# Second mixer: two linear-attention scores in one break of the weight stream, sparse-attention scores moved to the outputs' break

## The chip, the cores and the metric

One core of a Trainium2 chip runs the whole program; the other cores are idle. The metric is the device time of one execution in microseconds (us), less is better. TensorE (PE in the profile) multiplies, ScalarE (ACT) and VectorE (DVE) do the arithmetic between, GpSimd (POOL) prepares weights, and the SyncE queue (SP) streams weights in from memory.

## The reference

The model is two blocks of two layers each, on 256 tokens of width 1024. The first block has gated feed-forwards around an attention mixer. Each layer of the second block is a mixer of three branches and a squared-ReLU MLP:

```
z = rms_norm(x) @ w_in                      # split into the parts below
o_nsa = nsa_attention(...)                  # 8 heads, compressed + selected + windowed keys
o_gla = gated_linear_attention(...)         # 4 heads, decayed scores, state carried over tokens
o_mem = memory_attention(...)               # 4 heads into a memory of 256 tokens
merged = sum_b sigmoid(merge_b + b_merge) * (o_b @ w_branch[b])
x = x + merged @ w_out
x = x + square(relu(rms_norm(x) @ w_up)) @ w_down
```

The change touches only how the kernel orders work in this second mixer. In the gated linear attention the score of query i and key j is `sum_d q[i,d] k[j,d] exp(b[i,d] - b[j,d])` for j <= i, where b is the running sum of the log gates; the kernel computes it in 8 levels (pairs of tokens that lie 128, 64, ... 1 apart share a reference point), one matmul per level and head, and picks each score from its level by masks.

## The kernel before

**The stream.** All weights arrive as pieces of 128x1024 numbers through a ring (7 slots raw, 5 rounded). ACT rounds a piece (`hi`, L1352), POOL makes the rest (`lo`, L581), and PE multiplies every piece as three products, hi\*hi, hi\*lo and lo\*hi (L608 to L610), so that the result has fp32 accuracy. In the mixer a strip of 512 output columns consists of 4 pieces, and one piece is 12 matmuls of 512 columns. A strip accumulates in two PSUM banks, strip i in banks 2\*(i%2) and the next: so the two banks of strip i-1 lie idle during strip i, once they have been evicted.

**The breaks.** All other matmuls of the mixer stand between the pieces, in breaks. `mix2_work()` is a table written by hand: for each strip (the six `merge` strips, then `gr`) and each of its four pieces, the steps that follow the piece. Every engine's program walks the same table through `mix2_order()` and emits its own part of each step, so the table sets the order on PE, DVE and ACT at once; each engine's queue is in order.

**The steps.** `nsa_unit t` handles unit t of the sparse attention (17 of them, two heads each 64 wide, odd t and t+1 as a pair): PE makes the scores of a pair (`nsa_score`, lines of `pair_of_scores`, L852, into the banks SCORE = 4 and 5) at odd t, the transposes of unit t-1 (`turn_blocks`, L829, into bank TURNED = 6), and at even t the outputs of a pair (`nsa_outs`, L1186 and L839, into bank OUT = 7). DVE does in `nsa_unit t` at odd t: `minima(1)` on score bank 5, the copy of the transposed unit t-1 (`take_turned`, L2082), `minima(0)` on score bank 4 (both L2063), and `normalise` (L2070, L2074); at even t only the copy and `normalise`. `minima(0)` comes behind `take_turned` because it writes the slot that the transposes read.
`gla_unit hp t` handles the linear attention of head pair hp: t = 0, 1 are the two halves (4 levels each) of the scores of the first 128 tokens, t = 2, 3 those of the second 128 (8 instructions each, L1064), t = 2 with two more into TURNED (L1054). Both heads' scores go into the banks SCORE. `gla_out` (L1079, L1081) writes the outputs of a token tile into TURNED. DVE copies them out (L2352) and picks the scores (L2368). `decay hp i` prepares the decays on DVE and ACT.

**The waits.** `free[...]` in PE's program holds for each of the banks the semaphore that its last reader raises. So whoever writes SCORE next waits for `mn` (both minima) behind sparse scores, or for `gread` (the masks' picks) behind linear scores; whoever writes TURNED waits for `pt` (L2082) or `og` (L2352).

Of the kernel before, what the change touches and what calls it, by code (L numbers as in the profile page):

```python
# [19 lines left out]
P = 128  # L20
S = 256
MT = S // P
# [97 lines left out]
def mix2_work():  # L120
# [5 lines left out]
    gu = [[("gla_unit", hp, t) for t in range(5)] for hp in range(2)]  # L126
# [19 lines left out]
        ("rows", 2): ([nu[17]], [nu[18], gu[1][4]], [gla[3]], [gla[4], gla[5]]),  # L146
        ("rows", 0): (none, [gla[6]], [gla[7]], none),
        ("rows", 1): (none, none),
    }

# [440 lines left out]
def pe_program(M, V, sem):  # L591
# [5 lines left out]
    free = {0: None, 1: None, "turned": None, "out": None}  # L597
# [397 lines left out]
    def mix2(layer, c0, turn_next):  # L995
# [41 lines left out]
        def gla_score(hp, u):  # L1037
# [4 lines left out]
            wait_free(0)  # L1042
            wait_free(1)
# [3 lines left out]
            for hh, i in order:  # L1047
# [16 lines left out]
                t = pe.matmul(psum[:, SCORE[hh], i * P:i * P + P], lhsT, rhs, start=True, stop=True,  # L1064
                              skip_group_check=True)
            t.then_inc(sem["score"], 1)
            free[0] = free[1] = ("gread", 4 * nxt("gread"))
# [124 lines left out]
        for step in mix2_order():  # L1192
            what = step[0]
            if what == "strip":
                i, j = step[1:]
                name = names[i]
                if j == 0:
                    evicted(i)
                a_hi, a_lo = (y_hi, y_lo) if name in ("mk", "mv") else (h_hi, h_lo)
# [54 lines left out]
            elif what == "gla_unit":  # L1254
                hp, t = step[1:]
                if t in (2, 4):
                    gla_out(hp, t // 2 - 1)
                if t < 4:
                    gla_score(hp, t)
            elif what == "nsa":  # L1260
                nsa_step(step[1])
            elif what == "nsa_unit":
                t = step[1]
                if t == 0 or t % 2 and t < NSA_UNITS:
                    nsa_score(t)
                if t % 2 == 0 and t >= 4:
                    nsa_outs(t - 3)
                if 0 <= t - 1 < NSA_UNITS:
                    nsa_turn(t - 1)
            elif what == "rows":  # L1270
                b, i = step[1:]
                second = lambda: None
                if b == 2 and i == 0:
                    evicted(len(names))
# [579 lines left out]
def dve_program(M, V, sem):  # L1854
# [349 lines left out]
    def mix2(layer, c0, rstd):  # L2204
# [143 lines left out]
        def gla_unit(hp, t):  # L2348
            if t in (2, 4):
                m = t // 2 - 1  # L2350
                dve.wait_ge(sem["go"], nxt("go"))
                dve.tensor_copy(V.gqk[:, m, S * hp:S * hp + S], psum[:, TURNED, S:2 * S]).then_inc(sem["og"], 1)  # L2352
                n["og"] += 1
# [479 lines left out]
```

## Time and profile before

| | us |
|---|---|
| median of 3 runs | 1906.5 (1905.95 to 1906.9) |
| profiled execution | 1906.14, of which the span of its instructions 1904.6 |
| PE busy in the span | 1893.5 (99%) |
| POOL busy | 1563.4 (82%) |
| ACT busy | 1042.7 (55%) |
| DVE busy | 1029.4 (54%) |
| chain that ended last, PE's share | 96% |
| granted clock of PE | 1.0 |

A row of the timeline gives the start in us from the span's start, the duration, engine, line, operation, the tile written and the tiles read, and shapes; matmuls overlap in the pipeline, so it is the distance between starts that tells what one costs. `128*128`, `64*128` and `128*64` behind MATMUL are the rows and columns of the array that it uses. An fp32 matmul leaves two records where it runs as two passes, and the transposes one each. The two second mixers lie at about 1027 to 1228 us and 1486 to 1687 us of the span, up to the last branch; the part that the change touches is 1117 to 1212 us in the first and 1576 to 1671 us in the second.

### The profile page before, as it was taken

To read this page: it belongs to the slowest core of one execution; us is meant where nothing else is said; L and a number is where in the kernel's file an instruction comes from. 1 tells how busy PE (TensorE), PEld (TensorE's weight loads), DVE (VectorE), ACT (ScalarE), POOL (GpSimd) and SP (SyncE) were. 2 spreads that over 40 slices of the span, in tenths; PEclk is the share of its full clock that TensorE was granted. 3 is DMA by queue.
4 is the path that set the end of the run, shared out by engine and by line. 5 is a ranking of instruction groups with operands and counts; after the bars stand their busy time and mean duration, and the time that the engine had idled before them with its cause. 6 is when DMAs were issued, how large, how long until landed. Compare 5 with 4: busy or idle time off the path is not lost.

```text
span 1904.6 us, 26699 instructions
## 1 busy us (share of the span) xinstructions
PE 1893.5 (99%) x9356; PEld 1540.0 (81%) x9356; DVE 1029.4 (54%) x2621; ACT 1042.7 (55%) x1774; POOL 1563.4 (82%) x1136
## 2 busy tenths in 40 slices
PE   9999999999999999999999999999999999999999
PEld 7888777888888877788888877788888877788887
DVE  5438445444676745553453687547443477655553
ACT  6445666444644476554467444655446554556543
POOL 8988876988798877698879787779887968788986
PEclk9999999999999999999999999999999999999999
DMA  7665434666666543367657343456757533346664
GB/s 284 238 236 187 150 120 153 192 197 190 208 232 197 193 161 122 122 218 258 192 178 267 121 142 123 147 177 205 247 195 255 173 125 131 122 147 198 197 191 142
DMA packets 98385, 348.96 MB, mean 183 GB/s; under 512 B 13229, under 2 KB 13901, under 8 KB 97741
## 3 DMA queue, kind: packets, MB, share of 16 engines
q1 hardware_dynamic: 97676, 346.13, 54.9%
q8 instruction: 75, 1.23, 0.3%
q10 hardware_dynamic: 576, 1.14, 0.2%
q14 instruction: 58, 0.47, 0.1%
HBM read 346.17 MB, written 1.05 MB: 182 GB/s over the span
## 4 chain that ended last, share of the span: by engine, by line
PE 96%; DVE 2%; POOL 1%; ACT 0%; issue 0%; DMA 0%; SPq 0%; ACTq 0%; DVEq 0%
PE psum L608 29%; PE psum L610 28%; PE psum L609 28%; PE psum L829 1%; PE psum L839 1%; PE psum L677 1%; PE psum L852 1%; PE psum L1064 1%; POOL lo L581 1%; PE psum L819 1%; DVE psum L2024 1%; PE psum L875 0%; PE psum L916 0%; PE psum L726 0%; PE psum L1215 0%; PE psum L733 0%
## 5 line engine op out<-in xcount | busy, mean ns | idle before, releaser
L581 POOL TENSOR_TENSOR lo<-raw,hi 128x256 fp32r<-128x256 f32 (+2 forms) x1132 | 1563.2, 1404 | 328.1 <-ACT hi L1352 300.8
L1352 ACT ACTIVATE hi<-raw 128x1024 fp32r<-128x1024 f32 (+1 forms) x616 | 642.9, 1053 | 485.3 <-PE psum L610 446.3
L608 PE MATMUL psum<-hi,h_hi 128*128 128x512 f32 (+1 forms) x1600 | 634.2, 396 | 1.3 <-DVE h_lo L1913 0.9
L610 PE MATMUL psum<-hi,h_lo 128*128 128x512 f32 (+1 forms) x1600 | 622.1, 389 | 0.0
L609 PE MATMUL psum<-lo,h_hi 128*128 128x512 f32 (+1 forms) x1600 | 621.3, 388 | 0.0
L608 PEld LDWEIGHTS psum<-hi,h_hi 128*128 128x128 f32 x1600 | 301.3, 188 | 67.0 <-issue 3.4
L2024 DVE STREAM_TRANSPOSE psum<-big 32x128 f32<-32x128 f32 (+1 forms) x960 | 344.1, 358 | 14.2
L610 PEld LDWEIGHTS psum<-hi,h_lo 128*128 128x128 f32 x1600 | 300.5, 188 | 62.4
L609 PEld LDWEIGHTS psum<-lo,h_hi 128*128 128x128 f32 x1600 | 301.1, 188 | 57.7
L608 PE MATMUL psum<-hi,y_hi 128*128 128x512 f32 x832 | 328.4, 395 | 0.4 <-DVE y_lo L2033 0.4
L610 PE MATMUL psum<-hi,y_lo 128*128 128x512 f32 x832 | 324.6, 390 | 0.0
L609 PE MATMUL psum<-lo,y_hi 128*128 128x512 f32 x832 | 324.3, 390 | 0.0
L2033 DVE TENSOR_TENSOR y_lo<-psum,y_hi 128x512 fp32r<-128x512 f32 x76 | 51.0, 689 | 330.3 <-ACT y_hi L1478 330.1
L608 PEld LDWEIGHTS psum<-hi,y_hi 128*128 128x128 f32 x832 | 156.3, 188 | 35.9 <-issue 2.5
L610 PEld LDWEIGHTS psum<-hi,y_lo 128*128 128x128 f32 x832 | 156.3, 188 | 32.9
L609 PEld LDWEIGHTS psum<-lo,y_hi 128*128 128x128 f32 x832 | 156.5, 188 | 31.1
L1520 ACT ACTIVATE soft<-soft,small 128x128 f32<-128x128 f32 (+1 forms) x120 | 54.6, 456 | 129.9 <-DVE small L2063 109.0
L2012 DVE SCALAR_TENSOR_TENSOR big<-psum,small,big 128x256 f32<-128x256 f32 (+1 forms) x120 | 61.0, 551 | 86.8 <-ACT big L1468 86.8
L1468 ACT ACTIVATE big<-psum,small 128x256 f32<-128x256 f32 (+1 forms) x120 | 57.1, 528 | 53.8 <-PE psum L610 53.8
L1478 ACT ACTIVATE y_hi<-psum 128x512 fp32r<-128x512 f32 x76 | 42.7, 583 | 17.8 <-DVE psum L2024 17.6
L2082 DVE COPY soft<-psum 128x384 f32<-128x384 f32 (+2 forms) x68 | 35.4, 521 | 27.4 <-PE psum L829 27.4
L829 PE MATMUL psum<-consts,soft 128*128 128x128 f32 x188 | 34.3, 287 | 0.7 <-DVE soft L2074 0.7
(308 smaller groups left out, 1329.4 us busy)
## 6 DMA issues: line engine op xcount, KB each, us to landing
raw<-in_stream SPq DMA_DIRECT2D x608, 512.0 KB, 4.2
big<-in_w SPq DMA_DIRECT2D x14, 512.0 KB, 6.9
big<-in_post SPq DMA_DIRECT2D x6, 512.0 KB, 5.2
special<-in_b_merge SPq DMA_DIRECT2D x2, 1536.0 KB, 8.1
raw<-in_stream SPq DMA_DIRECT2D x8, 296.0 KB, 5.8
memkv<-in_mem_turned SPq DMA_DIRECT2D x2, 1024.0 KB, 6.0
big<-in_band SPq DMA_DIRECT2D x2, 768.0 KB, 6.7
big<-in_x_turned SPq DMA_DIRECT2D x2, 512.0 KB, 5.9
```

What stands on the lines that cost most here:

```text
L581: t = pool.tensor_tensor(M.lo[:, slot, w], M.raw[:, slot, w], f32(M.hi[:, slot_hi, w]), ALU.subtract)
L608: pe.matmul(out, lhs_hi, rhs_hi, start=start, stop=False)
L609: pe.matmul(out, lhs_hi, rhs_lo, start=False, stop=False)
L610: return pe.matmul(out, lhs_lo, rhs_hi, start=False, stop=stop)
L829: t = pe.transpose(psum[:, TURNED, i * P:i * P + P], soft[:, slot, 0, col:col + P], V.ident)
L1352: act.activation(M.hi[:, slot_hi, used], M.raw[:, slot, used], ACT.Copy).then_inc(sem["hi"], 1)
L1468: t = act.activation(act_s[:, m, :], psum[:, bank + m, 0:width], ACT.Silu if gated else ACT.Relu, scale=V.scale[:, m:m + 1])
L1478: act.activation(flat(y_hi[:, kt:kt + 2, :]), psum[:, bank + g, :], ACT.Copy).then_inc(sem["yhi"], 1)
L1520: t = act.activation(out, prob[:, w], ACT.Exp, scale=-1.0, bias=mn[:, i:i + 1], accum_out=total[:, i:i + 1])
L2012: t = dve.scalar_tensor_tensor(prod_s[:, m, :], psum[:, bank + m, col:col + width], V.scale[:, m:m + 1], act_s[:, m, :], ALU.mult, ALU.mult)
L2024: t = dve.transpose(dst[32 * b:32 * b + 32, :, :, 32 * a:32 * a + 32], src[32 * a:32 * a + 32, :, :, 32 * b:32 * b + 32])
L2033: dve.tensor_tensor(flat(y_lo[:, kt:kt + 2, :]), psum[:, bank + g, :], f32(flat(y_hi[:, kt:kt + 2, :])), ALU.subtract).then_inc(sem["ylo"], 1)
```

## The change

Four things change, in both second-mixer layers.

1. The five `gla_unit` steps of a head pair become three. Step m makes both halves of the scores of token tile m (16 instructions, 18 for m = 1) in one go, behind the outputs of tile m-1. They stand in the break behind the second piece of a strip, behind an odd `nsa_unit` in the same break. Four breaks of a head pair (pieces 0, 2 of two strips, with `gla_out` in the third) become two, and the breaks behind pieces 0 and 2 of these strips are gone.
2. The first half's scores go to SCORE as before. The second half's go to the idle pair of strip banks, `idle_banks(strip)`: PE waits until the strip before has been evicted, and the strip that comes next into these banks waits until DVE has picked the scores.
3. Sparse scores of units 5, 7, ... 15 move from the odd `nsa_unit` to the even one before it, between its outputs and its transposes. The odd units keep only their transposes on PE. DVE's order within a unit is as before.
4. The outputs of the second token tile of head pair 0 move from the break of `nsa_unit` 8 to that of `nsa_unit` 9, ahead of the transposes; those of head pair 1 stay.

```diff
@@ mix2_work
-        ("merge", 2): ([gu[0][0]], [nu[5]], [gu[0][1]], [nu[6]]),
-        ("merge", 3): ([gu[0][2]], [nu[7]], [gu[0][3]], [gu[0][4], nu[8], decay[1][0]]),
-        ("merge", 4): ([nu[9], decay[1][1]], [nu[10], decay[1][2]], [nu[11], decay[1][3]], [nu[12]]),
-        ("merge", 5): ([gu[1][0]], [nu[13]], [gu[1][1]], [nu[14]]),
-        "gr": ([gu[1][2]], [nu[15]], [gu[1][3]], [nu[16]]),
+        ("merge", 2): (none, [nu[5], gu[0][0]], none, [nu[6]]),
+        ("merge", 3): (none, [nu[7], gu[0][1]], none, [nu[8], decay[1][0]]),
+        ("merge", 4): ([gu[0][2], nu[9], decay[1][1]], [nu[10], decay[1][2]], [nu[11], decay[1][3]], [nu[12]]),
+        ("merge", 5): (none, [nu[13], gu[1][0]], none, [nu[14]]),
+        "gr": (none, [nu[15], gu[1][1]], none, [nu[16]]),
...
+def idle_banks(strip):
+
+    return 2 - 2 * (strip % 2), 3 - 2 * (strip % 2)
...
@@ pe_program, gla_score
             pe.wait_ge(sem["eb"], n["eb"])
-            wait_free(0)
-            wait_free(1)
+            banks = idle_banks(strip) if part else SCORE
+            if part:
+                evicted(strip + 1)
+                wait_free("idle")
+            else:
+                wait_free(0)
+                wait_free(1)
...
@@ pe_program, the steps
-                if t == 0 or t % 2 and t < NSA_UNITS:
+                if t in (0, 1, 3):
                     nsa_score(t)
                 if t % 2 == 0 and t >= 4:
                     nsa_outs(t - 3)
+                    if t + 1 < NSA_UNITS:
+                        nsa_score(t + 1)
                 if 0 <= t - 1 < NSA_UNITS:
                     nsa_turn(t - 1)
...
@@ dve_program, gla_unit
-                                              queries(psum[:, 4:6, i * P:i * P + P])))
+                                              queries(psum[:, bank:bank + 2, i * P:i * P + P])))
```

What PE runs for the first token tile of a head pair. Before, strip `merge 2`, with stream pieces at the dots (L1064 linear scores, L852 sparse scores, L829 transposes):

```order
L1064 MATMUL psum<-memkv,big 128x128 [waits s_mn,s_eb]
L1064 MATMUL psum<-memkv,big 128x128 x7
...
L852 MATMUL psum<-kT,qT 128x128 [waits s_gread,s_qk]
L852 MATMUL psum<-kT,qT 128x128
L852 MATMUL psum<-kT,qT 128x256 x2
L829 MATMUL psum<-consts,soft 128x128 [waits s_pt,s_prob]
L829 MATMUL psum<-consts,soft 128x128 x2
...
L1064 MATMUL psum<-memkv,big 128x128 [waits s_mn,s_eb]
L1064 MATMUL psum<-memkv,big 128x128 x5
```

Now, one break (L834 are the transposes and L1074 the linear scores in the new numbering, L613 the stream):

```order
L834 MATMUL psum<-consts,soft 128x128 [waits s_pt,s_prob]
L834 MATMUL psum<-consts,soft 128x128 x2
L1074 MATMUL psum<-memkv,big 128x128 [waits s_mn,s_eb]
L1074 MATMUL psum<-memkv,big 128x128 x7
L1074 MATMUL psum<-memkv,big 128x128 [waits s_z_merge,s_eb]
L1074 MATMUL psum<-memkv,big 128x128 x5
L1074 MATMUL psum<-big,kT 128x128 x2
L613 MATMUL psum<-hi,h_hi 128x512 [waits s_lo]
```

Three breaks have become one, and the first linear score now stands directly behind the transposes, still with its wait for `mn`.

The second token tile on PE. Before, strip `merge 3`, first break (L1079 is `gla_out`, L1054 the two additional scores):

```order
L1079 MATMUL psum<-big 128x128 [waits s_pt,s_z_gv,s_gread]
L1079 MATMUL psum<-big 128x128
L1064 MATMUL psum<-memkv,big 128x128 [waits s_gread,s_eb]
L1064 MATMUL psum<-memkv,big 128x128 x3
L1054 MATMUL psum<-memkv,big 128x128 [waits s_og]
L1064 MATMUL psum<-memkv,big 128x128 x4
L1054 MATMUL psum<-memkv,big 128x128 [waits s_rowtile]
```

Now (L1093 is `gla_out`, L1064 the two additional scores):

```order
L834 MATMUL psum<-consts,soft 128x128 [waits s_pt,s_prob]
L834 MATMUL psum<-consts,soft 128x128 x2
L1093 MATMUL psum<-big 128x128 [waits s_pt,s_z_gv,s_gread]
L1093 MATMUL psum<-big 128x128
L1074 MATMUL psum<-memkv,big 128x128 [waits s_mn,s_eb]
L1074 MATMUL psum<-memkv,big 128x128 x3
L1064 MATMUL psum<-memkv,big 128x128 [waits s_og]
L1074 MATMUL psum<-memkv,big 128x128 x4
L1064 MATMUL psum<-memkv,big 128x128 [waits s_rowtile]
L1074 MATMUL psum<-memkv,big 128x128 [waits s_z_merge,s_eb]
```

The transposes stand directly ahead of `gla_out`, which writes the same bank, and the first scores wait for `mn` where they waited for `gread`.

DVE around the same place. Before (L2352 copies the outputs, L2361 the two additional scores, L2368 picks):

```order
L2352 COPY big<-psum 128x256 [waits s_go]
L2361 COPY extra<-psum 128x256 [waits s_score]
L2368 COPY_PREDICATED big<-special,psum 128x2x64
...
L2063 ISA soft,small<-psum,consts 128x128 [waits s_pturn,s_score,s_gread]
...
L2082 COPY soft<-psum 128x384 [waits s_o,s_pturn]
L2063 ISA soft,small<-psum,consts 128x128 [waits s_pturn,s_score]
...
L2070 RECIPROCAL small<-small 128x2 [waits s_exp]
L2074 TENSOR_SCALAR soft<-soft,small,extra 128x128 [waits s_dve]
```

Now (L2104 is the copy of the transposes, L2085 the minima, L2092 and L2096 `normalise`, L2372 the copy of the outputs):

```order
L2104 COPY soft<-psum 128x384 [waits s_o,s_pturn]
L2085 ISA soft,small<-psum,consts 128x128 [waits s_pturn,s_score]
...
L2092 RECIPROCAL small<-small 128x2 [waits s_exp]
L2096 TENSOR_SCALAR soft<-soft,small,extra 128x128 [waits s_dve]
L2096 TENSOR_SCALAR soft<-soft,small,extra 128x256
L2372 COPY big<-psum 128x256 [waits s_go]
L2384 COPY extra<-psum 128x256 [waits s_score]
```

The copy of the outputs now stands behind the whole DVE part of the sparse unit in the same break.

## Rows read from the trace of the kernel before

**Rows 1.** The page, busy time, share and instructions by engine.
```profile
PE 1893.5 (99%) x9356; PEld 1540.0 (81%) x9356; DVE 1029.4 (54%) x2621; ACT 1042.7 (55%) x1774; POOL 1563.4 (82%) x1136
```

**Rows 2.** Who waited for whom, PE: total us, times, longest us.
```profile
PE psum L839 <- DVE soft L2082: 1.2, 2, 0.7
PE psum L829 <- DVE soft L2074: 0.7, 2, 0.4
...
PE psum L608 <- POOL lo L581: 0.4, 2, 0.2
```

**Rows 3.** Timeline of PE, a break with transposes alone: start, duration, what.
```profile
1106.88 0.39 PE L609 MATMUL psum<-lo,h_hi 128*128 128x512 f32 x1
1107.11 0.39 PE L610 MATMUL psum<-hi,h_lo 128*128 128x512 f32 x1
1107.34 0.49 PE L829 MATMUL psum<-consts,soft 128*128 128x128 f32 x3
...
1107.90 0.40 PE L609 MATMUL psum<-lo,h_hi 128*128 128x512 f32 x1
```

**Rows 4.** Timeline of PE, a break with sparse scores and transposes.
```profile
1110.21 0.39 PE L610 MATMUL psum<-hi,h_lo 128*128 128x512 f32 x1
1110.53 0.93 PE L852 MATMUL psum<-kT,qT 64*128 64x128 f32 x8
1111.38 0.55 PE L829 MATMUL psum<-consts,soft 128*128 128x128 f32 x3
...
1112.00 0.39 PE L609 MATMUL psum<-lo,h_hi 128*128 128x512 f32 x1
```

**Rows 5.** Timeline of PE, two breaks with linear scores alone (first token tile).
```profile
1121.49 0.39 PE L610 MATMUL psum<-hi,h_lo 128*128 128x512 f32 x1
1121.81 1.16 PE L1064 MATMUL psum<-memkv,big 64*128 64x128 f32 x16
1122.90 0.50 PE L608 MATMUL psum<-hi,h_hi 128*128 128x512 f32 x1
1123.24 0.39 PE L609 MATMUL psum<-lo,h_hi 128*128 128x512 f32 x1
...
1129.93 0.94 PE L1064 MATMUL psum<-memkv,big 64*128 64x128 f32 x12
1130.71 0.39 PE L1064 MATMUL psum<-big,kT 64*128 64x128 f32 x4
1131.03 0.50 PE L608 MATMUL psum<-hi,h_hi 128*128 128x512 f32 x1
```

**Rows 6.** Timeline of PE, outputs of the first tile, then scores of the second.
```profile
1137.92 0.60 PE L1079 MATMUL psum<-big 128*128 128x128 f32 x4
1138.46 0.71 PE L1064 MATMUL psum<-memkv,big 64*128 64x128 f32 x8
1139.05 0.37 PE L1054 MATMUL psum<-memkv,big 64*128 64x128 f32 x1
```

**Rows 7.** Timeline of PE and DVE, end of transposes and start of their copy.
```profile
1153.26 0.55 PE L829 MATMUL psum<-consts,soft 128*128 128x128 f32 x3
...
1153.85 0.56 DVE L2082 COPY soft<-psum 128x384 f32<-128x384 f32 x1 [0.80 <-PE psum L829]
```

**Rows 8.** Timeline of DVE, the DVE part of an odd sparse unit.
```profile
1144.62 0.55 DVE L2082 COPY soft<-psum 128x384 f32<-128x384 f32 x1
...
1145.63 0.08 DVE L2063 DVE_READ_ACCUMULATOR2_ANT small<- 128x1 f32 x1
...
1145.83 0.68 DVE L2074 TENSOR_SCALAR soft<-soft,small,extra 128x128 f32<-128x128 f32 x2
```

**Rows 9.** Timeline of DVE, the two scalings of unit 5, when they took longest.
```profile
1128.67 1.47 DVE L2074 TENSOR_SCALAR soft<-soft,small,extra 128x128 f32<-128x128 f32 x2
```

**Rows 10.** Timeline of DVE, the copy of the linear outputs.
```profile
1138.57 0.42 DVE L2352 COPY big<-psum 128x256 f32<-128x256 f32 x1 [0.88 <-PE psum L1079]
```

**Rows 11.** Timeline of PE, outputs of `nsa_unit` 12.
```profile
1169.68 0.88 PE L839 MATMUL psum<-soft,big 128*64 128x128 f32 x12 [0.49 <-DVE soft L2082]
```

More of the change, by code:

```diff
@@ L125, in mix2_work @@
     mu = [("mem_unit", t) for t in range(6)]
-    gu = [[("gla_unit", hp, t) for t in range(5)] for hp in range(2)]
+    gu = [[("gla_unit", hp, m) for m in range(MT + 1)] for hp in range(2)]
     decay = [[("decay", hp, i) for i in range(4)] for hp in range(2)]
@@ L595, in pe_program @@
     n = Counter()
-    free = {0: None, 1: None, "turned": None, "out": None}
+    free = {0: None, 1: None, "turned": None, "out": None, "idle": None}
     def nxt(name, k=1):
@@ L1035, in mem_out, with gla_score @@
             free["out"] = ("y2lo", nxt("y2lo"))
-        def gla_score(hp, u):
+        def gla_score(hp, u, strip):
             m, part = u // 2, u % 2
@@ L1063, in gla_score @@
                     lhsT, rhs = V.gla_k[hp][half, toks], V.gla_q[hp][half, toks]
-                t = pe.matmul(psum[:, SCORE[hh], i * P:i * P + P], lhsT, rhs, start=True, stop=True,
+                t = pe.matmul(psum[:, banks[hh], i * P:i * P + P], lhsT, rhs, start=True, stop=True,
                               skip_group_check=True)
             t.then_inc(sem["score"], 1)
-            free[0] = free[1] = ("gread", 4 * nxt("gread"))
+            read = ("gread", 4 * nxt("gread"))
+            if part:
+                free["idle"] = read
+            else:
+                free[0] = free[1] = read
             if u == 2:
@@ L1198, in mix2 @@
                     evicted(i)
+                    wait_free("idle")
+                    free["idle"] = None
+                    strip_now = i
                 a_hi, a_lo = (y_hi, y_lo) if name in ("mk", "mv") else (h_hi, h_lo)
@@ L1254, in mix2 @@
             elif what == "gla_unit":
[L1255 to L1259, printed above, removed]
+                hp, m = step[1:]
+                if m:
+                    gla_out(hp, m - 1)
+                if m < MT:
+                    for u in (2 * m, 2 * m + 1):
+                        gla_score(hp, u, strip_now)
             elif what == "nsa":
@@ L1273, in mix2 @@
                 if b == 2 and i == 0:
+                    wait_free("idle")
+                    free["idle"] = None
                     evicted(len(names))
@@ L2346, in taken, with gla_out, gla_unit @@
             dve.wait_ge(sem["gread"], nxt("gread"))
[L2348 to L2353, printed above, removed]
-            if t < 4:
-                part = t % 2
-                if hp == 0 and t == 0:
-                    own(dve.memset(V.att_flat, 0.0))
+        def gla_out(hp, m):
+            dve.wait_ge(sem["go"], nxt("go"))
+            dve.tensor_copy(V.gqk[:, m, S * hp:S * hp + S], psum[:, TURNED, S:2 * S]).then_inc(sem["og"], 1)
+            n["og"] += 1
+        def gla_unit(hp, step, strip):
+            if step:
+                gla_out(hp, step - 1)
+            if hp == 0 and step == 0:
+                own(dve.memset(V.att_flat, 0.0))
+            for part in range(2 if step < MT else 0):
+                bank = idle_banks(strip)[0] if part else SCORE[0]
                 dve.wait_ge(sem["score"], nxt("score"))
-                if t == 2:
+                if step and not part:
                     dve.tensor_copy(V.att_off_flat, psum[:, TURNED, 0:S])
@@ L2500, in mix2 @@
             what = step[0]
-            if what == "memory_in":
+            if what == "strip":
+                strip_now = step[1]
+            elif what == "memory_in":
                 for pair in (2 * step[1], 2 * step[1] + 1):
@@ L2563, in mix2 @@
             elif what == "gla_unit":
-                gla_unit(*step[1:])
+                gla_unit(*step[1:], strip_now)
             elif what == "nsa":
```

2 lines of the change are left out of this document (1 added, 1 removed).

## The prediction

> **What bounds the kernel now.** I read the page first: PE is busy 99% of the span [rows 1], so a step is worth what it adds to PE's queue, and the 54% of DVE matter only where PE waits. The list of waits came next: PE waits for DVE 1.9 us in four places and for POOL 0.4 us in two [rows 2]. So neither weights nor arithmetic hold PE up today, and there is next to nothing to win from waits; what can be won is PE's own time in the breaks. Then the timeline of PE through merge 2 to gr. A stream matmul follows the next by 0.23 us (1106.88, 1107.11) [rows 3]. I measure a break from the last stream matmul before it to the second one behind it, less two such steps (0.455 us), because the first matmul behind a break is always late. Last, the timeline of DVE beside it, for when a bank comes free. The same pattern stands 459 us later in the second layer, so I work out one layer and double it.
>
> **What the breaks cost by shape.** Transposes alone: 1107.90 - 1107.11 - 0.455 = 0.335 us [rows 3]. Sparse scores and transposes: 1112.00 - 1110.21 - 0.455 = 1.335 us, so the scores add 1.00 [rows 4]. Linear scores, half a tile: 1123.24 - 1121.49 - 0.455 = 1.295 us [rows 5]. Inside, a pair of records (two heads side by side) takes 0.11 us: six pairs take 0.78, two pairs and the way back to the stream 0.32, all eight 1.09 to 1.10 [rows 5]. That is 8 x 0.111 = 0.89 plus 0.1 in and 0.1 out; the rest of 1.295 lies in the stream matmuls on either side, 0.32 instead of 0.23 before and 0.34 instead of 0.23 behind. So every change between the full array and half of it costs about 0.2 us.
>
> **What the change removes, per layer.**
> - The second half of the linear scores follows the first without a change of shape: it adds 0.89 instead of 1.295. Four times (two tiles, two head pairs): 4 x 0.405 = 1.6 us.
> - The first half, behind transposes instead of in its own break: 0.23 + 0.33 (three transposes) + 0.10 + 1.09 + 0.34 - 0.455 = 1.63, and apart 0.335 + 1.295 = 1.63. Nothing. The 0.10 is the change of shape behind outputs: four records from 1137.92, scores at 1138.46, 0.54 = 4 x 0.11 + 0.10 [rows 6].
> - Six sparse scores (units 5 to 15) stand between outputs and transposes. From their first record to the transposes is 1111.38 - 1110.53 = 0.85 us [rows 4], where they cost 1.00 in a break with the transposes: 6 x 0.15 = 0.9 us. The outputs use half the columns (128\*64), the scores half the rows (64\*128), and no break of today puts these two side by side. I take the same 0.2 us for that change as rows 5 give for one to the full array. Bounds: no change at all, 0.65 each and 1.2 us more won; twice the price, 1.2 us less.
> - The outputs of tile 1 of pair 0 move from one break to the next with no change of shape on either side: nothing.
>
> Together 2.5 us a layer, with bounds 1.3 and 3.7. For the sparse scores the Trainium skill has a rule, TensorEngine Tiling (Array Packing), Key Properties: going to another tiling mode drains the array, going to another tile of the same mode does not. Rows 5 agree (0.2 us in and out, none between the heads' halves), and by the rule the untried change from columns to rows drains too, which is the 0.9 us; without a drain that term would be 2.1 us.
>
> **What it adds: waits in the same break.** Today a bank written by one break is read by DVE during the next pieces. The change puts writer and next writer side by side. I set 0 at the last stream matmul before the break.
>
> (c) Tile 0, twice a layer. The transposes start at 0.23 and the linear scores could start at 0.66. They write bank 4, which holds the sparse scores of unit 6 (14) until `minima(0)`, and DVE does `minima(0)` behind the copy of these very transposes. The transposes end 0.49 behind their start [rows 3], at 0.72; the copy starts 0.04 later (1153.81, 1153.85) [rows 7], at 0.76; the minima end 1.09 behind the start of the copy (1144.62, 1145.63 + 0.08) [rows 8], at 1.85; PE follows 0.06 us behind DVE (copy to 1138.99, L1054 at 1139.05) [rows 6, 10]. So the scores start at 1.91: a wait of 1.25 us. Bounds 1.0 (the first of the accumulators suffices) and 1.35.
>
> (a) Tile 1, twice a layer, three waits in a row. `gla_out` writes the bank of the transposes: it may start when their copy is done, 0.76 + 0.55 + 0.06 = 1.37 instead of 0.56, a wait of 0.81. Its scores then start at 1.37 + 0.54 = 1.91, just when the minima are done. The additional scores L1054 come 0.59 behind (1138.46, 1139.05) [rows 6], at 2.50, and need the copy of the outputs. But DVE's queue has the copy of the outputs behind `normalise`: scalings from 0.76 + 1.21 = 1.97 [rows 8], which last 0.68 to 1.47 us [rows 8, 9]; I take the middle, next start at 2.98. Copy 0.42 and 0.06: 3.46, a wait of 0.96 (0.55 to 1.4). Together 1.77, bounds 1.36 and 2.2.
>
> (b) `nsa_unit` 9, once a layer. Its transposes stand directly behind `gla_out` and need its copy: outputs end, 0.04 to the copy, 0.42, 0.06, so 0.53 from 1138.52 to 1139.05 [rows 6, 10], where they would have followed 0.16 before that end: 0.69 us. Today sparse outputs of 0.8 us lie between and hide it. DVE's decays of pair 1 (four operations behind `nsa_unit` 8) end about when the outputs do; bounds 0.55 and 1.0.
>
> What does not wait: the second half's idle banks (the strip before is evicted over 5 us earlier), the next strip in them (DVE needs some 7 us from the break's start for all picks, PE comes back after 9), and the scores moved ahead of the transposes (their banks' minima are two pieces old).
>
> (d) `nsa_unit` 12 waits today for DVE, whose decays fill its queue: 0.49 us for a copy in layer 0 [rows 11], and then for the scalings, 1.9 us over both layers [rows 2]. The chain of DVE through units 8 to 11 stays as it is, some 0.6 us later by (b); the sparse scores now lie between outputs and transposes and hide the second of these waits. I take 1.0 us off for both layers together; bounds 0 and 1.9.
>
> **The sum.** 2 x (2 x 1.25 + 2 x 1.77 + 0.69 - 2.5) - 1.0 = 2 x 4.23 - 1.0 = 7.5 us. The profiled execution took 1906.14 us (span 1904.6): 1913.6; the median of the runs is 0.4 us higher. I say 1913.5 us, 0.4% slower. All low bounds: 2 x (2.0 + 2.72 + 0.55 - 3.7) - 1.9 = 1.2 us; all high: 2 x (2.7 + 4.4 + 1.0 - 1.3) = 13.6 us.
>
> **Rivals.**
> 1. Faster, 1899 us. DVE's answers cost PE nothing: the point is whether `minima(0)` and the copies are done before the next writer's turn. If DVE had them by then, only the 2.5 us a layer and the 1.9 us of today's waits would be left, 2 x 2.5 + 1.9 = 6.9 us. For it: DVE is idle nearly half of the time, and it would be enough to have another piece between. Against: the copy needs the transposes of the same break, and PE's queue is in order. Chance 0.07.
> 2. No change, 1907 to 1910. The waits are there but short: the change from outputs to scores does not drain (2.4 us less), scalings take 0.68 us (0.4 less, four times), and today's waits go altogether. 7.5 - 2.4 - 1.6 - 0.9 = 2.6 us, 1908.7. For it: six places with an unseen change of shape. Chance 0.20.
> 3. Slower by more, 1917 to 1920: DVE, pushed back by (b), delays the outputs of unit 12 more than now, then the transposes of unit 13 (it has some 0.4 us to spare there), and the scores behind them; with 1.5 us in each of two places a layer, 7.5 + 4 to 6. Chance 0.10.
> 4. The second half cannot use the idle banks in time and waits for the eviction or its reader: then the merged break is split by a wait of up to the 1.4 us of the eviction. Nothing in the order makes DVE late there. Inside the others' chances.
>
> **The numbers.** Forecast 1913.5 with chance 0.63 for 1910 to 1917. About 0.2% (3.8 us) is what a measurement of this kernel can tell from no change. Slower: 0.63 and 0.10, of which I move 0.03 to the middle for its lower end, 0.70. Same: 0.20 and 0.03, 0.23. Faster: 0.07. The range 1905.5 to 1917.5 leaves out the first rival and most of the third.
>
> **What would show it.** In the new profile PE's waits for DVE grow from 1.9 to some 14 us: the linear scores wait 1.2 us for L2085 (minima) twice a layer, `gla_out` 0.8 us for L2104, L1064 about 1 us for L2372, the transposes of unit 9 some 0.5 us for L2372. The step between a linear score pair stays 0.11 us throughout the merged break, there are 8 breaks fewer a layer, and the sparse scores take 0.85 us between outputs and transposes. If PE's waits stay near 2 us, the forecast is wrong and the first rival right. POOL and ACT keep their order and lead; a wait of PE for `lo` would be a cause I did not count.

## The result, and the profile after

The changed kernel takes 1915.59 us, the median of six runs, against 1906.24 us for the kernel before in as many runs on the same chip. The ratio is 1.005, interval [1.004, 1.006]: slower by 9.35 us, where 7 us were forecast. The six runs lie in two groups: 1913.93, 1913.96 and 1914.27 us with a granted TensorE clock of 1.0, and 1916.90, 1917.37 and 1917.78 us with a mean clock of 0.998. The profiled execution is the slowest of them (1917.78 us, span 1916.3), so a part of what its trace shows beyond the one before is the clock, told of below.

The page, busy time by engine. It answers to [rows 1]:

```profile
PE 1894.9 (99%) x9356; PEld 1544.2 (81%) x9356; DVE 1029.7 (54%) x2621; ACT 1043.1 (54%) x1774; POOL 1563.6 (82%) x1136
```

The numbers of instructions are those of before, and so are the busy times within 1.4 us (4.2 on PEld). The span is 11.7 us longer, so about 10 us are time in which PE stands idle. (Its share still reads 99%: 12 us are 0.6% of the span.)

The list of waits of PE, against [rows 2]: who waited for whom, total us, times, longest:

```profile
PE psum L1074 <- issue: 5.0, 4, 1.2
PE psum L1093 <- DVE soft L2104: 3.0, 4, 0.7
PE psum L1064 <- DVE big L2372: 2.1, 4, 0.9
PE psum L834 <- DVE big L2372: 1.2, 2, 0.6
PE psum L844 <- DVE soft L2104: 1.1, 2, 0.6
...
PE psum L613 <- POOL lo L586: 0.4, 2, 0.2
```

These five are 12.4 us, where the prediction had some 14; before, the waits for DVE in this part were 1.9 us. Each stands at the place the prediction gave it. The first is the wait (c) and is put down to "issue", since the profile sees no releaser; DVE's timeline below shows that it ends with the minima. The wait for `lo` is unchanged: POOL has no part in it.

Timeline of PE and DVE, first token tile of head pair 0 in the first layer:

```profile
1125.66 0.39 PE L615 MATMUL psum<-hi,h_lo 128*128 128x512 f32 x1
1125.90 0.49 PE L834 MATMUL psum<-consts,soft 128*128 128x128 f32 x3
...
1126.42 0.56 DVE L2104 COPY soft<-psum 128x384 f32<-128x384 f32 x1 [2.46 <-PE psum L834]
...
1127.45 0.08 DVE L2085 DVE_READ_ACCUMULATOR2_ANT small<- 128x1 f32 x1
...
1127.63 1.83 PE L1074 MATMUL psum<-memkv,big 64*128 64x128 f32 x28 [1.25 <-issue]
...
1129.62 0.50 PE L613 MATMUL psum<-hi,h_hi 128*128 128x512 f32 x1
```

The reader is to see the chain: transposes end, copy 0.56, minima, last accumulator read at 1127.45 + 0.08, first score 0.10 later. The wait is 1.25 us. From the first score to the stream are 1.99 us for 32 records; the second half follows the first without a pause, though it writes other banks.

Second token tile of the same head pair:

```profile
1142.60 0.39 PE L615 MATMUL psum<-hi,h_lo 128*128 128x512 f32 x1
1142.83 0.49 PE L834 MATMUL psum<-consts,soft 128*128 128x128 f32 x3
...
1144.06 0.68 PE L1093 MATMUL psum<-big 128*128 128x128 f32 x4 [0.74 <-DVE soft L2104]
1144.58 1.13 DVE L2096 TENSOR_SCALAR soft<-soft,small,extra 128x128 f32<-128x128 f32 x2
...
1145.63 0.41 DVE L2372 COPY big<-psum 128x256 f32<-128x256 f32 x1
1146.09 0.37 PE L1064 MATMUL psum<-memkv,big 64*128 64x128 f32 x1 [0.70 <-DVE big L2372]
...
1146.97 0.42 PE L1064 MATMUL psum<-memkv,big 64*128 64x128 f32 x1
...
1147.18 0.42 PE L1064 MATMUL psum<-memkv,big 64*128 64x128 f32 x1
...
1149.24 0.79 PE L613 MATMUL psum<-hi,h_hi 128*128 128x512 f32 x1
```

Both waits of (a) are there, 0.74 us for the copy of the transposes and 0.70 us for the copy of the outputs, which starts only when the scalings (1.13 us) are through. And something that was not forecast: behind the second wait a pair of score records takes 0.21 us (1146.97 to 1147.18) where it took 0.11 before [rows 5]. The view by stretches shows why; PEclk is the third number from the end (width, then busy time and instructions of PE, PEld, DVE, ACT and POOL, PEclk, DMA share, GB/s):

```profile
1143.00:1146.00 3.00, 1.65 (x15) 1.12 (x13) 2.61 (x9) 1.84 (x5) 2.86 (x5) 1.00 0.49 182
1146.00:1149.00 3.00, 2.91 (x28) 2.91 (x28) 1.30 (x6) 0.09 (x1) 2.86 (x5) 0.58 0.00 0
1149.00:1152.00 3.00, 3.00 (x14) 2.29 (x13) 1.90 (x5) 0.00 (x0) 0.21 (x1) 0.85 0.00 0
...
1609.00:1612.00 3.00, 2.06 (x25) 1.87 (x24) 1.36 (x4) 1.12 (x3) 2.86 (x5) 0.79 0.18 71
1612.00:1615.00 3.00, 3.00 (x20) 2.55 (x19) 2.66 (x8) 0.00 (x0) 1.47 (x3) 0.64 0.02 5
```

A mean clock of 0.58 and then 0.85 means that (0.42 + 0.15) x 3 / 0.5 = 3.4 us were run at the lower of its two levels, 1.2 instead of 2.4 GHz. Before it, PE was busy 1.65 of 3.00 us. The same place of the second layer has it too, (0.21 + 0.36) x 3 / 0.5 = 3.4 us. Nowhere else in the second mixers, and nowhere there in the kernel before, does the clock fall.

The second token tile of head pair 1, at full clock:

```profile
1198.60 0.39 PE L615 MATMUL psum<-hi,h_lo 128*128 128x512 f32 x1
...
1200.06 0.68 PE L1093 MATMUL psum<-big 128*128 128x128 f32 x4 [0.74 <-DVE soft L2104]
...
1200.58 0.67 DVE L2096 TENSOR_SCALAR soft<-soft,small,extra 128x128 f32<-128x128 f32 x2
1201.16 0.42 DVE L2372 COPY big<-psum 128x256 f32<-128x256 f32 x1
...
1201.63 0.37 PE L1064 MATMUL psum<-memkv,big 64*128 64x128 f32 x1 [0.24 <-DVE big L2372]
...
1203.49 0.50 PE L613 MATMUL psum<-hi,h_hi 128*128 128x512 f32 x1
```

Here the scalings take 0.67 us and the wait is 0.24. (POOL had ended its last `lo` operation at 1200.30, while such operations ran beside the scalings of 1.13 us; experiment 1 has more on this.) From L1064 to the stream are 1.86 us; in the tile of head pair 0, most of it at half clock, 3.15. That difference, 1.29, and 0.32 more until the stream is back in its step of 0.23 are 1.6 us for each fall.

Last, the sparse scores, now between outputs (L844) and transposes (unit 6):

```profile
1135.30 0.88 PE L844 MATMUL psum<-soft,big 128*64 128x128 f32 x12
1136.11 0.93 PE L857 MATMUL psum<-kT,qT 64*128 64x128 f32 x8
1136.97 0.55 PE L834 MATMUL psum<-consts,soft 128*128 128x128 f32 x3
```

0.86 us from scores to transposes; 0.85 was forecast. This step has a change from half the rows to the full array, as in [rows 4]. The change that no break of before had, from half the columns to half the rows, lies one step earlier, from outputs to scores: 1136.11 - 1135.30 = 0.81 us. In the same unit of the kernel before, the outputs went straight to the transposes, from half the columns to the full array:

```profile
1133.97 0.88 PE L839 MATMUL psum<-soft,big 128*64 128x128 f32 x12
1134.78 0.55 PE L829 MATMUL psum<-consts,soft 128*128 128x128 f32 x3
```

That is 0.81 us too. So the unseen change costs what the one to the full array costs, as the forecast assumed.

### The profile page after: what moved, and what is told of

Its sections match the earlier page's. It is cut to its first block, busy times and chain, and to the rows that moved or that the text cites. A ratio compares the mean times of both kernels' runs of the same rounds, so it can differ in the third digit from the quotient of the medians.

```text
span 1916.3 us, 26709 instructions
## 1 busy us (share of the span) xinstructions
PE 1894.9 (99%) x9356; PEld 1544.2 (81%) x9356; DVE 1029.7 (54%) x2621; ACT 1043.1 (54%) x1774; POOL 1563.6 (82%) x1136
## 3 DMA queue, kind: packets, MB, share of 16 engines
q8 instruction: 75, 1.23, 0.3%
## 4 chain that ended last, share of the span: by engine, by line
PE 95%; DVE 3%; ACT 1%; issue 1%; POOL 1%; ACTq 0%
PE psum L613 28%; PE psum L615 28%; PE psum L614 28%; PE psum L834 1%; PE psum L844 1%; PE psum L682 1%; PE psum L857 1%; PE psum L1074 1%; POOL lo L586 1%; PE psum L824 1%; DVE psum L2046 1%; PE psum L880 0%; PE psum L921 0%; PE psum L731 0%; PE psum L738 0%
## 5 line engine op out<-in xcount | busy, mean ns | idle before, releaser
L613 PE MATMUL psum<-hi,h_hi 128*128 128x512 f32 (+1 forms) x1600 | 632.9, 396 | 1.3 <-DVE h_lo L1935 0.9
L613 PEld LDWEIGHTS psum<-hi,h_hi 128*128 128x128 f32 x1600 | 301.2, 188 | 67.4 <-issue 3.9
L613 PE MATMUL psum<-hi,y_hi 128*128 128x512 f32 x832 | 328.1, 394 | 0.4 <-DVE y_lo L2055 0.4
L613 PEld LDWEIGHTS psum<-hi,y_hi 128*128 128x128 f32 x832 | 156.2, 188 | 36.1 <-issue 2.5
L2104 DVE COPY soft<-psum 128x384 f32<-128x384 f32 (+2 forms) x68 | 35.5, 522 | 53.2 <-PE psum L834 53.2
L2096 DVE TENSOR_SCALAR soft<-soft,small,extra 128x128 f32<-128x128 f32 x64 | 34.6, 582 | 1.2
```

Of the source, the lines that this page charges most:

```text
L613: pe.matmul(out, lhs_hi, rhs_hi, start=start, stop=False)
L2104: dve.tensor_copy(soft[:, slot, 1, 0:width], psum[:, TURNED, 0:width]).then_inc(sem["pt"], 1)
```

## The experiments

All eight kernels compute the whole reference. I give the median and the ratio to the kernel before, which took 1906.2 to 1906.4 us in the runs made beside them. Where a break is compared, it is measured as in the prediction, or by its gap: from the last stream matmul before it to the first behind it, less one step of 0.23.

**1. The pairs in a break of their own.** The rival of the whole story is that the merged break or the new order of the sparse scores is itself slow. This kernel keeps the merged pairs, gives them a break of their own, the first of their strip, and puts the sparse scores back where they were.

```diff
-        ("merge", 2): (none, [nu[5], gu[0][0]], none, [nu[6]]),
-        ("merge", 3): (none, [nu[7], gu[0][1]], none, [nu[8], decay[1][0]]),
-        ("merge", 4): ([gu[0][2], nu[9], decay[1][1]], ...
+        ("merge", 2): ([gu[0][0]], [nu[5]], none, [nu[6]]),
+        ("merge", 3): ([gu[0][1]], [nu[7]], none, [gu[0][2], nu[8], decay[1][0]]),
+        ("merge", 4): ([nu[9], decay[1][1]], ...
...
-                if t in (0, 1, 3):
+                if t == 0 or t % 2 and t < NSA_UNITS:
                     nsa_score(t)
                 if t % 2 == 0 and t >= 4:
                     nsa_outs(t - 3)
-                    if t + 1 < NSA_UNITS:
-                        nsa_score(t + 1)
```

("merge", 5) and "gr" are changed in the same way.

> Both halves of the linear scores in one break with the second half in the idle strip banks, as in the changed kernel, but in a break of their own behind the strip's first piece; sparse scores in the odd units and the second tile's outputs in unit 8's break, as before the change. Theory (the halves together win 0.4 us each, the loss comes from waits that the new neighbours bring): four merges a layer of 0.405 us, no new wait, so 2 x 1.6 = 3.2 us under the kernel before: 1903.0 us, PE's waits for DVE near today's 1.9 us, granted clock 1.0 throughout. Rival (the merged break or the idle banks are themselves what costs): about as slow as the changed kernel, or at least not under 1906.

Measured: 1904.88 us (1904.69 to 1905.70, 11 runs), ratio 0.9993 [0.9984, 1.0001]; the interval just reaches no change. So the waits come from the place, not from the merging: against the changed kernel 10.7 us go. But only 1.5 of the 3.2 us of savings arrive. The merged break has the expected size; the rest is in new waits around unit 11:

```profile
PE psum L834 <- DVE soft L2094: 2.1, 4, 0.7
PE psum L844 <- DVE soft L2102: 1.4, 2, 0.7
```

DVE did not come earlier with PE. Its timeline, with the four decays behind unit 8:

```profile
1154.48 3.02 DVE L2351 TENSOR_TENSOR big<-extra 128x256 f32<-128x256 f32 x4
1157.42 0.28 DVE L2083 CUSTOM_DVE_ANT_0 soft<-psum,consts 128x128 f32<-128x128 f32 x1
```

and the same rows of the kernel before:

```profile
1155.52 1.95 DVE L2331 TENSOR_TENSOR big<-extra 128x256 f32<-128x256 f32 x4
1157.43 0.29 DVE L2063 CUSTOM_DVE_ANT_0 soft<-psum,consts 128x128 f32<-128x128 f32 x1
```

DVE starts its decays 1.04 us earlier, and they take 3.02 instead of 1.95 us and end at the same time, 1157.42. POOL's `lo` operations run without a pause until 1156.19 in the kernel before and 1156.88 here, so three of the four decays start beside them instead of one. Two more groups of four in the kernel before, the first with POOL at work and the second without:

```profile
1100.41 3.58 DVE L2331 TENSOR_TENSOR big<-extra 128x256 f32<-128x256 f32 x4
...
1159.80 1.43 DVE L2331 TENSOR_TENSOR big<-extra 128x256 f32<-128x256 f32 x4
```

All 32 decays of that kernel fall into two kinds: the 22 that start with no `lo` operation running take 0.41 or 0.42 us, the ten that start beside one 0.94 to 0.96. In experiment 1 it is 18 and 14, with the same times. No experiment removed POOL's work, but the rows leave no decay that goes the other way.

**2. The pairs one piece later.** The order of the sparse scores as in the change, but one piece of the stream between transposes and linear scores, and likewise between `gla_out` and unit 9.

```diff
-        ("merge", 2): (none, [nu[5], gu[0][0]], none, [nu[6]]),
-        ("merge", 3): (none, [nu[7], gu[0][1]], none, [nu[8], decay[1][0]]),
-        ("merge", 4): ([gu[0][2], nu[9], decay[1][1]], [nu[10], decay[1][2]], ...
-        ("merge", 5): (none, [nu[13], gu[1][0]], none, [nu[14]]),
-        "gr": (none, [nu[15], gu[1][1]], none, [nu[16]]),
+        ("merge", 2): (none, [nu[5]], [gu[0][0]], [nu[6]]),
+        ("merge", 3): (none, [nu[7]], [gu[0][1]], [nu[8], decay[1][0]]),
+        ("merge", 4): ([nu[9], decay[1][1]], [gu[0][2], nu[10], decay[1][2]], ...
+        ("merge", 5): (none, [nu[13]], [gu[1][0]], [nu[14]]),
+        "gr": (none, [nu[15]], [gu[1][1]], [nu[16]]),
```

> The changed kernel, but its merged linear scores one piece later, in a break of their own, and the second tile's outputs of head pair 0 at the head of unit 10's break, ahead of sparse outputs, scores and transposes, instead of directly ahead of unit 9's transposes. Sparse scores stay between outputs and transposes. Theory: all savings of the change (2.5 us a layer) without the waits (a), (b) and (c), and today's waits in unit 12 a bit smaller (1 us): 1906.2 - 5 - 1 = 1900.2 us, no fall of the clock. Rival (sparse scores in the outputs' break cost by themselves, through a change of shape that is dearer than 0.2 us or through the DVE): above 1903, that is above the kernel with the pairs in their own break and sparse scores left alone.

Measured: 1902.86 us (1902.42 to 1903.24, 11 runs), ratio 0.9982 [0.9973, 0.9991]: 3.5 us under the kernel before and 12.7 under the changed one. Of the expected saving 2.7 us are missing. Two waits hold most of them, 2.7 us together, of which the expectation had counted about 0.9:

```profile
PE psum L1128 <- DVE big L2334: 1.4, 2, 0.7
PE psum L844 <- DVE soft L2104: 1.3, 2, 0.7
```

The second is unit 12's, which DVE's decays delay. The first is new. I read it so that the transposes of the linear outputs behind the strip `gr` come one piece closer to DVE's last picks; no run takes it away.

**3. The copy ahead of the scalings.** Here the change stays; on DVE alone the copy of the outputs moves ahead of `normalise`, so that the second wait of (a) should go, and little else.

```diff
@@ dve_program, gla_unit
-            if step:
+            if step == 2:
                 gla_out(hp, step - 1)
@@ dve_program, nsa_unit
+                if t in (7, 15):
+                    gla_out(t // 15, 0)
                 normalise(t % 2, SEG, [V.gates[:, m, at:at + 1] for m in range(MT)])
```

> The changed kernel, but DVE copies the first tile's linear outputs before the scaling (normalise) of the sparse unit in the same break instead of behind it. Theory: the wait of the additional scores for that copy (0.7 to 0.94 us, four times) nearly goes, since the copy can start when the minima are done and the outputs are there: 2.5 to 3.3 us less. If the clock's fall behind that break comes from PE's idle time in it, both falls go as well (about 1.75 us each in the profile): 1909 to 1911 us and equal runs. Rival (the fall is tied to something else, the long run of small matmuls or the place): clock still at half for 3.4 us there, and runs still apart by up to 4 us.

Measured: 1911.90 us (1911.66 to 1912.23, 7 runs), ratio 1.0029 [1.0018, 1.0041]. This is 2.1 us under the faster group of the changed kernel, as much as the wait for L2372 summed to, and 5.5 us under the other group. It is also 0.9 us above the range that was expected. By the breaks 2.5 us are saved beside the clock; in return PE's waits for `lo` are 1.0 us in this trace instead of 0.4. The clock is 1.0 in all seven runs. The same break of head pair 0:

```profile
1143.18 0.68 PE L1093 MATMUL psum<-big 128*128 128x128 f32 x4 [0.74 <-DVE soft L2104]
1143.80 0.71 PE L1074 MATMUL psum<-memkv,big 64*128 64x128 f32 x8
1144.38 0.37 PE L1064 MATMUL psum<-memkv,big 64*128 64x128 f32 x1
...
1146.24 0.50 PE L613 MATMUL psum<-hi,h_hi 128*128 128x512 f32 x1
```

L1064 follows the scores by 0.58 us with no wait, and from there to the stream are 1.86 us as in head pair 1.

**4. The waits filled with work.** Is it the idle time of PE that lowers the clock, or what it computes there? This kernel has all the waits of the change, but PE multiplies constants into idle banks meanwhile: three full-array matmuls ahead of `gla_out` and three pairs of halves ahead of the additional scores. Their results are not used.

```diff
+        def fill(strip, times, halves):
+            for _ in range(times):
+                for hh in range(2 if halves else 1):
+                    rows = slice(64 * hh, 64 * hh + 64) if halves else slice(0, P)
+                    pe.matmul(psum[:, idle_banks(strip)[hh], 0:P], V.ident[rows], V.ident[rows], start=True, stop=True,
...
                     if not hh:
+                        fill(strip, 3, True)
                         wait_free("turned")
...
+                if m == 1:
+                    evicted(strip_now + 1)
+                    wait_free("idle")
+                    fill(strip_now, 3, False)
                 if m:
                     gla_out(hp, m - 1)
```

> The changed kernel with dummy matmuls in the waits of the second tile's break: three of 128 columns on the full array (0.67 us) ahead of the linear outputs, and three pairs on half arrays (0.67 us) ahead of the additional scores, into the idle strip banks that the second half's scores overwrite. They take no more time than PE waits there. Theory (the clock falls since PE stands idle there): no fall of the clock, about 1914 us in every run, the time of the changed kernel's fast group (1913.9 to 1914.3). Rival (the fall comes from the work, not from the idle time): clock at half as before, 1914 to 1918. If the dummies cost time by themselves, 1916 with a clock of 1.0.

Measured: 1914.53 us (1914.30 to 1914.61, 5 runs), ratio 1.0043 [1.0030, 1.0055], clock 1.0 in every run. With the same chain of waits and more work, the kernel lands 0.6 us above the faster group of the changed kernel and never in the other one. The stretches of its trace, as above:

```profile
1143.00:1146.00 3.00, 2.83 (x34) 2.36 (x34) 2.37 (x9) 1.93 (x5) 2.86 (x5) 1.00 0.52 175
1146.00:1149.00 3.00, 3.00 (x31) 2.61 (x29) 2.28 (x7) 0.00 (x0) 2.62 (x4) 1.00 0.03 5
```

So the fall comes with the idle time of PE, not with what it computes. In experiment 3, where only the first of the two waits was left, the clock did not fall either. The runs are few: if each had an even chance of a fall, as in the changed kernel, five without one would come once in 32 times and seven once in 128.

**5. The third kernel with the outputs one piece later**, which takes the wait (b) away: `[gu[0][2], nu[9], decay[1][1]], [nu[10], ...` becomes

```diff
+        ("merge", 4): ([nu[9], decay[1][1]], [gu[0][2], nu[10], decay[1][2]], [nu[11], decay[1][3]], [nu[12]]),
```

> As the kernel with the copy ahead of the scaling (1911.9 us), but the second tile's linear outputs of head pair 0 at the head of unit 10's break instead of directly ahead of unit 9's transposes. It takes wait (b) away alone. Theory: 0.69 us a layer less on PE, 1910.5 us, if it is not given back. Rival (DVE's chain of copies and decays through units 9 to 12 is what ends the wait of unit 12, so PE only comes earlier to it): the wait of unit 12 grows from 0.6 to about 1.2 us and the time stays within 0.4 us of 1911.9.

Measured: 1909.33 us (1908.77 to 1910.14, 11 runs), ratio 1.0017 [1.0008, 1.0026]: 2.57 us under experiment 3, where 1.4 was expected. The gap of unit 9's break falls from 1.94 to 0.25 us, and that of unit 10's rises from 2.06 to 2.95, the outputs' own time: 0.8 us a layer. Most of the rest is unit 12, whose gap falls from 3.12 to 2.78 us, 0.7 us in both layers. I had left that out: the copy of the outputs no longer pushes DVE's chain of decays back.

**6. The third kernel with tile 0 one piece later**, which takes the wait (c) away and nothing else.

```diff
-        ("merge", 2): (none, [nu[5], gu[0][0]], none, [nu[6]]),
-        ("merge", 5): (none, [nu[13], gu[1][0]], none, [nu[14]]),
+        ("merge", 2): (none, [nu[5]], [gu[0][0]], [nu[6]]),
+        ("merge", 5): (none, [nu[13]], [gu[1][0]], [nu[14]]),
```

> As the kernel with the copy ahead of the scaling (1911.9 us), but the first token tile's linear scores of both head pairs one piece later in a break of their own. It takes wait (c) away alone, for minima that stand behind the copy of the same break's transposes. Theory: four times 1.25 us less, 1906.9 us. Rival (part of it comes back in later waits for DVE, as with the pairs in their own break): 1907.5 to 1909.

Measured: 1906.43 us (1906.06 to 1907.06, 11 runs), ratio 1.0001 [0.9992, 1.0010]: 5.5 us under experiment 3, 5.0 expected. No wait of L1074 is left, the other waits stay, and the merged pair stands between two stream pieces:

```profile
1127.71 0.39 PE L615 MATMUL psum<-hi,h_lo 128*128 128x512 f32 x1
1128.03 1.83 PE L1074 MATMUL psum<-memkv,big 64*128 64x128 f32 x28
1129.70 0.39 PE L1074 MATMUL psum<-big,kT 64*128 64x128 f32 x4
1130.02 0.50 PE L613 MATMUL psum<-hi,h_hi 128*128 128x512 f32 x1
1130.36 0.39 PE L614 MATMUL psum<-lo,h_hi 128*128 128x512 f32 x1
```

It takes 1130.36 - 1127.71 - 0.455 = 2.195 us, where two breaks of half a tile take 2 x 1.295 [rows 5]: 0.395 saved, 0.405 forecast.

**7. The second kernel with the sparse scores at the odd units**, as before the change (the second part of experiment 1's diff). It measures what their move to the outputs is worth where nothing waits for the linear scores.

> As the kernel with the pairs one piece later (1902.9 us), but with the sparse scores back in the odd units, ahead of their transposes. It takes the third part of the change away alone. Theory: the sparse scores win 0.15 us each in the outputs' break, 0.9 us a layer, and hide one of the two waits of unit 12 for DVE (about 0.4 us): back in the odd units the kernel is 2 x 1.3 = 2.6 us slower, 1905.5 us. Rival (their place is worth nothing, since DVE's chain through units 8 to 12 sets the pace there and takes back what PE wins): within 0.7 us of 1902.9.

Measured: 1904.12 us (1903.89 to 1904.84, 11 runs), ratio 0.9989 [0.9981, 0.9998], 1.26 us over experiment 2. That is half of the 2.6 expected, which was too much to begin with: by the gaps of the breaks the move is worth 1.25 + 1.20 apart less 2.06 + 0.25 together, 0.14 us each, twelve times, 1.7 to 1.8 us, the term of the prediction. Of that, unit 12 takes 0.9 us back: it waits 0.15 and 0.40 us here against 0.63 and 0.80 in experiment 2. That leaves 0.9 us. The rest lies in the piece behind unit 4's break: PE's weights wait there for `lo` from POOL, and the piece takes 0.26 us longer in each layer, 0.5 in both, which brings the sum to 1.4 (1.5 between the spans of the two profiles).

**8. The decays spread.** The second kernel, with DVE's last two decay steps of head pair 1 one break later each, to take unit 12's wait away.

```diff
-        ("merge", 4): (..., [gu[0][2], nu[10], decay[1][2]], [nu[11], decay[1][3]], [nu[12]]),
-        ("merge", 5): (none, [nu[13]], [gu[1][0]], [nu[14]]),
+        ("merge", 4): (..., [gu[0][2], nu[10]], [nu[11], decay[1][2]], [nu[12]]),
+        ("merge", 5): ([decay[1][3]], [nu[13]], [gu[1][0]], [nu[14]]),
```

> As the kernel with the pairs one piece later, but the last two decay steps of head pair 1 stand one and two pieces later (behind unit 11, and behind the first piece of merge 5), since their reader now comes later too. Theory (what PE wins in merge 4 is given back in unit 12, whose break waits for DVE's copies behind the decays, 0.6 to 0.9 us a layer in the traces of both new kernels): that wait goes, 1.2 to 1.6 us less: 1901.4 us. Rival (the end of the strip gr, where the transposes of the linear outputs wait 0.7 us a layer for DVE, takes it up instead): 1902.9 as before, with that wait grown.

Measured: 1901.22 us (1900.99 to 1901.70, 9 runs), ratio 0.9974 [0.9964, 0.9984]. It is the fastest of all, 5.0 us under the kernel before and 14.4 under the changed one. Unit 12's wait is gone (gap 2.49 us in both layers). Of waits that the kernel before did not have, one is left, that of L1128 from experiment 2, 1.5 us over both layers.

## Why the prediction was right, and where it was not

The forecast was 1913.5 us, slower; measured were 1915.59, and 1913.96 in the runs in which the clock did not fall. The terms for both layers, by the breaks of the profiled execution (time of a break in which nothing waits taken from experiments 6 and 8, where the same break stands alone):

| term | forecast, us | measured, us |
|---|---|---|
| savings (linear pairs, sparse scores) | -5.0 | -5.1 |
| (c) tile 0, four times | +5.0 | +5.2 |
| (a) tile 1, four times | +7.1 | +6.4, and 3.2 for the clock |
| (b) unit 9, twice | +1.4 | +1.6 |
| (d) unit 12's wait | -1.0 | -1.0 |
| sum | +7.5 | +7.1, and 3.2 |

The profiled span is 11.7 us longer; 10.3 of it stand between the first and the last of these breaks, and about 0.6 had gathered ahead of the first. The row of savings is taken so that the sum meets these 10.3 us. Break by break the savings are 8 x 0.395 + 12 x 0.145 = 4.9 us. The other 0.2 lies in the stream: it steps by about 0.23 us just behind a break and by 0.227 later, and there are 16 breaks fewer.

- **Savings.** Right in both parts: 0.395 for a pair against 0.405, 0.14 to 0.15 us for a move of the sparse scores against 0.15. The choice that had to be made blind was whether rows beside columns cost a change of shape. They do: without it each move would have won 0.35. The Trainium skill's rule (TensorEngine Tiling (Array Packing), Key Properties), that a change of tiling mode drains the array, agrees with this, and the rival "no change" loses its main support, 2.4 us. What the prediction does not say is that its rows for 0.85 hold the way from the scores to the full array only; the unseen change is the way into them, 0.81 us from the outputs. Experiment 7 adds that 0.9 of these 1.8 us can be eaten by a wait of a later unit.
- **(c).** The scores start 1127.63 - 1125.66 = 1.97 us behind the last stream matmul; 1.91 was forecast. Experiment 6 takes this term alone away and wins 5.5 us.
- **(a).** The place and the order of the waits were right; the size of the last was not known. The additional scores start 3.49 and 3.03 us behind the last stream matmul in the first layer (1146.09 and 1201.63) and 3.73 and 3.03 in the second, against 3.46. The scalings decide it, 1.13, 0.67, 1.36 and 0.67 us; the forecast took the middle of 0.68 and 1.47 for all four, which is 0.5 us too much in the sum, most of the 0.7 that the term is off. The long ones run beside POOL's `lo` operations, the short ones do not. Experiment 3 confirms that the copy's place in DVE's queue makes this wait: moved ahead, it costs nothing.
- **(b)** 0.61 us of wait against 0.69; by the break it is 0.8 us. Experiment 5 shows that its effect reaches further than its own break, to unit 12.
- **(d)** Before, unit 12's breaks had 1.01 and 1.23 us over an unhindered one, after 0.64 and 0.63. The estimate of 1.0 off for both held, as forecast: the wait for the scalings [rows 2] is hidden, and the one for the copy is about as long as before, 1.1 us over both layers for 1.2.
- **What failed** is the step of the sum by which a wait costs PE its own length and no more. At the second tile of head pair 0 the two waits of (a) follow each other so closely that the clock falls, and the work behind them runs at half speed for 3.4 us. That costs 1.6 us each by the breaks and (1917.37 - 1913.96) / 2 = 1.7 us by the middle runs of the two groups; it puts the median 2 us above the forecast. Nothing in the trace before could show it, since there the clock never fell in this part. But the sum itself had PE standing twice within 3 us, and I did not ask what that does to the clock. That the median is only 2 us off is in part luck: three of six runs had the falls, so half of their 3.4 us counts, and the 0.7 us too much in (a) takes some of that back.
- **The rivals.** The first (faster) needed DVE's answers to be free; its conditions are met in experiments 2 and 8, by one piece in between, and it then gives 3.5 and 5.0 us, not 6.9, because DVE's chain gives a part back. The second fell with the change of shape. The third, a cascade through units 12 and 13, did not come; that the slower runs lie in its range has another cause. The fourth did not come either: the merged pair has no step at its middle.

## What to carry to other kernels

A wait moved into the break of the work that releases it is paid in full, however idle the waited-for engine is: count the chain of copy, reduction and handover (here 1.25 us) against the drains saved (here 0.4), and try one piece of other work in between first, which turned a loss of 9 us into a gain of 3. When a saving arrives short, look for the next place where the same slow engine is needed; here two decays moved by one break gave 1.6 us back. Two waits of PE close together can cost more than their sum, so read the granted clock in the stretch behind them.

## What the runs showed of the hardware

- **The clock fell behind two waits of 0.74 and 0.70 us** (0.94 in the second layer), with PE busy 1.65 of 3.00 us, and stayed at 1.2 GHz for 3.4 us. It fell in this trace in both layers, and three of six runs show the same mean clock of 0.998, three none. It did not fall behind (c), with one wait of 1.25 us and this stretch:

```profile
1125.00:1128.00 3.00, 1.75 (x14) 1.34 (x14) 1.54 (x7) 1.15 (x5) 2.86 (x5) 1.00 0.66 229
```

nor at head pair 1 (0.74 and 0.24 us), nor where constants were multiplied in the waits. What decides between the two groups of runs was not settled. The Trainium skill (TensorE: Matmul & The Clock Gate, What's actually happening) says that the gate follows how busy PE has been, which experiments 3 and 4 agree with. By the formula in its section Back-to-back issue gap, for a matmul taken alone, 128 columns take 0.107 us at the low level and 0.056 at the high one. The ratio, 1.9, is that of this case, but the times are not: a pair takes 0.21 and 0.11 us here, twice as long. The two of a pair start 0.01 us apart and not one behind the other, and a record on the full array takes 0.11 us as well [rows 6].
- **Going from half the columns to half the rows costs as much as going to the full array**: from the first output to the first sparse score is 0.81 us, and from the same output to the transposes of before also 0.81. Each of the twelve moves of sparse scores wins 0.14 to 0.15 us, where 0.15 was worked out with that price of about 0.2 us and 0.35 without it.
- **The same operation of DVE takes 0.42 or 0.95 us, by whether POOL is at work when it starts.** The decays subtract 128x256 numbers in SBUF; in the kernel before, 22 of 32 start with POOL idle and take 0.41 or 0.42 us, ten start beside one of its `lo` operations and take 0.94 to 0.96. A group of four took 1.43, 1.95, 3.02 or 3.58 us by how many of them met POOL, and two scalings 0.67 us without it and up to 1.36 beside it. To price a chain of DVE, look at what POOL does at that time.
